# TensorE's program for the twelve later experts of a mixture-of-experts stage, written out in place of a loop of four rounds

## The reference, cut to what matters

```python
y = jnp.zeros_like(h)
for e in range(N_EXPERTS):                         # 16 experts
    a = jax.nn.silu(h @ w_gate[e]) * (h @ w_up[e])  # (t, 1024) @ (1024, 512)
    y = y + gates[:, e:e + 1] * (a @ w_down[e])     # (t, 512) @ (512, 1024)
```

## Time and profile before

| what | value |
|---|---|
| time, three runs | 1175.56, 1176.21, 1176.38 us, median 1176.21 |
| the profiled execution: its own time | 1178.95 us |
| the profiled execution: span, first to last instruction | 1177.1 us |
| mean granted TensorE clock | 0.927 |
| TensorE busy in the span | 983.2 us (84%), of these 368.7 us in the MoE products (L1906) |
| TensorE idle before MoE products, ended by up weights | 47.6 us |
| TensorE idle before MoE products, ended by nothing the profile shows ("issue") | 20.8 us in 12 waits |
| MoE products of layer 0 and of layer 1, in the span | 423.1 to 664.5 us, and 935.3 to 1148.1 us |

### The profile page before, as it was taken

How to read it: one execution, slowest core, us unless ns; L and a number is a source line. 1 busy time by engine, 2 the same in 40 slices (tenths; PEclk the granted TensorE clock), 3 DMA queues, 4 the chain that set the end, 5 groups by cost and what they waited for, 6 DMA issues and landing times.

```text
span 1177.1 us, 24444 instructions
## 1 busy us (share of the span) xinstructions
PE 983.2 (84%) x9596; PEld 652.9 (55%) x9597; DVE 402.6 (34%) x811; ACT 377.5 (32%) x806; POOL 217.6 (18%) x329
## 2 busy tenths in 40 slices
PE   3799999988899989799898569999999779876650
PEld 1477777544555656456566357887555546553430
DVE  1533331357833532122122373123744512121103
ACT  3433321466832222122122354224743112221102
POOL 0000000000000033344344201910000224342211
PEclk8799999999999889899999879999999889997775
DMA  9766664998230749999999467225447698999972
GB/s 340 254 215 217 222 216 176 344 361 322 92 163 36 281 170 372 421 423 422 422 422 399 168 224 169 72 72 187 171 145 312 256 415 354 421 422 425 427 302 113
DMA packets 93682, 322.07 MB, mean 274 GB/s; under 512 B 21241, under 2 KB 33954, under 8 KB 81330
## 3 DMA queue, kind: packets, MB, share of 16 engines
q1 hardware_dynamic: 85746, 305.40, 67.2%
q0 software_dynamic: 7008, 12.62, 2.9%
q10 hardware_dynamic: 864, 3.15, 0.7%
HBM read 313.67 MB, written 13.99 MB: 278 GB/s over the span
## 4 chain that ended last, share of the span: by engine, by line
PE 67%; DMA 17%; DVE 7%; issue 4%; ACT 3%; SPq 1%; POOL 1%; POOLq 0%; DVEq 0%; ACTq 0%
PE ps L1906 23%; PE ps L1667 21%; DMA expert_sets<-in_moe_w_up_dram 10%; PE ps L1822 7%; PE ps L1570 5%; PE ps L1594 4%; DMA ring<-in_ada_w_dram 2%; DMA ada_late<-in_ada_w_dram 2%; DMA expert_rows<-moe,scatter_idx 1%; PE ps L1749 1%; PE ps L1778 1%; PE ps L1722 1%; PE ps L1877 1%; DMA moe<-h_rows,gather_idx 1%; DMA val<-expert_rows 1%
## 5 line engine op out<-in xcount | busy, mean ns | idle before, releaser
L1906 PE MATMUL ps<-expert_sets,moe 128*32 128x256 f32 x6304 | 368.7, 396 | 78.1 <-DMA expert_sets<-in_moe_w_up_dram 47.6
L1906 PEld LDWEIGHTS ps<-expert_sets,moe 128*32 128x32 f32 x6304 | 235.1, 114 | 211.1 <-issue 98.1
L1528 DVE STREAM_TRANSPOSE moe<-moe 128x256 f32<-128x256 f32 x70 | 45.8, 654 | 316.1 <-PE ps L1906 294.2
L1667 PE MATMUL ps<-w_high,x_high 128*128 128x512 f32 x352 | 142.8, 406 | 6.6 <-DVE hT L508 3.0
L1667 PE MATMUL ps<-w_high,x_low 128*128 128x512 f32 x352 | 139.1, 395 | 0.0
L1667 PE MATMUL ps<-w_low,x_high 128*128 128x512 f32 x352 | 139.1, 395 | 0.0
L1083 ACT ACTIVATE moe<-ps 128x128 f32<-128x128 f32 x68 | 18.9, 277 | 261.9 <-PE ps L1906 259.7
L475 DVE TENSOR_TENSOR w_low<-ring,w_high 128x2048 fp32r<-128x2048 f32 x24 | 56.1, 2345 | 132.0 <-ACT w_high L472 132.0
L751 POOL MEMSET moe<- 128x128 f32 x2 | 0.4, 204 | 541.1 <-PE ps L1848 541.1
L774 POOL DMA_INDIRECT expert_rows<-moe,scatter_idx x74 | 75.8, 1024 | 78.7 <-POOL scatter_idx L811 57.9
L1667 PEld LDWEIGHTS ps<-w_high,x_high 128*128 128x128 f32 x352 | 67.4, 191 | 30.6 <-issue 17.4
(11 more groups left out here) (236 smaller groups left out, 1108.7 us busy)
## 6 DMA issues: line engine op xcount, KB each, us to landing
expert_sets<-in_moe_w_down_dram SPq DMA_DIRECT2D x32, 2048.0 KB, 19.3
expert_sets<-in_moe_w_gate_dram SPq DMA_DIRECT2D x30, 2048.0 KB, 18.8
expert_sets<-in_moe_w_up_dram SPq DMA_DIRECT2D x30, 2048.0 KB, 21.8
ring<-in_ada_w_dram SPq DMA_DIRECT2D x16, 2048.0 KB, 8.1
ring<-in_diff_w_qkv_dram SPq DMA_DIRECT2D x6, 2048.0 KB, 8.1
ada_late<-in_ada_w_dram SPq DMA_DIRECT2D x6, 2048.0 KB, 13.0
ring<-in_na_w_qkv_dram SPq DMA_DIRECT2D x6, 2048.0 KB, 8.9
rows<-mod_rows SPq DMA_DIRECT2D x12, 512.0 KB, 8.7
```

The costliest lines, as they stand in the source:

```text
L1528: dve.transpose(blk_inT, blk_in[b].rearrange("p (j k) -> p k j", k=KC)).then_inc(m_xt[l], 1)
L1667: mm = pe.matmul(ps[:, n % 2], x_part[:, k, tok], w_part, start=(k == 0 and i == 0), stop=(k == KC - 1 and i == 2))
L1906: mm = pe.matmul(ps[g * SLOTS:(g + 1) * SLOTS, bank, 0:n_out], lhs_T[:, k, :], weights(k, g), start=(k == 0), stop=(k == n_chunks - 1), sk ...
```

## The change

In TensorE's program, experts 1 to 15 are now all written out with a Python loop that calls `expert` with the number of the expert; the `pe.Fori` of four rounds is gone. The end of an expert's blocks is loaded in the program of the expert before (`then=p + 1`) with a fixed address, and kept in a register of the list `ends`; the two loads at the head of each round are gone. Expert 3, which loaded no end, now loads that of expert 4. `gates_loaded` and `down_loaded` lose their argument `rounds`. The programs of the other four engines are as they were, and so are the products, the weights and their order.

```diff
-                def gates_loaded(p, rounds=0):
+                def gates_loaded(p):
                     nth, per_layer = nth_load(0, p)
                     for w in range(2):
-                        pe.wait_ge(m_wl[gate_set(p)][w], 16 * (nth + rounds + l * per_layer))
+                        pe.wait_ge(m_wl[gate_set(p)][w], 16 * (nth + l * per_layer))
-                def down_loaded(p, rounds=0):
+                def down_loaded(p):
                     nth, per_layer = nth_load(2, p)
-                    pe.wait_ge(m_wl[p % 3][2], 16 * (nth + rounds + l * per_layer))
+                    pe.wait_ge(m_wl[p % 3][2], 16 * (nth + l * per_layer))
-                def expert(p, first, end, rounds=0, then=None):
+                def expert(p, first, end, then=None):
...
-                for p in range(1, 4):
-                    ends.append(expert(p, ends[p - 1], ends[p], then=p + 1 if p < 3 else None))
-                with pe.Fori(0, (N_EXP - 4) // 3) as three:
-                    end_0, end_1 = block_end(3 * three + 3), block_end(3 * three + 4)
-                    end_2 = expert(4, end_0, end_1, three, 3 * three + 5)
-                    end_3 = expert(5, end_1, end_2, three, 3 * three + 6)
-                    expert(6, end_2, end_3, three)
+                for p in range(1, N_EXP):
+                    ends.append(expert(p, ends[p - 1], ends[p], then=p + 1 if p + 1 < N_EXP else None))
```

More of the change, by code:

```diff
@@ L1942, in expert @@
                     else:
-                        gates_loaded(p, rounds)
+                        gates_loaded(p)
                     gates_ups(first, gate_set(p))
                     after = None if then is None else block_end(then)
-                    down_loaded(p - 1, rounds)
+                    down_loaded(p - 1)
                     downs(first - 1, (p - 1) % 3)
                     with pe.If(first + 1 < end):
-                        down_loaded(p, rounds)
+                        down_loaded(p)
                         pe.sem_inc(s_turn_pe, 1)
```

## The result

The changed kernel takes 1186.68 us (median of 4 runs, 1184.25 to 1188.06) against 1176.3 us (1175.56 to 1177.66) for the kernel before: ratio 1.0074, 95% interval 1.0050 to 1.0098. I had predicted 1177.1 and a range up to 1182.0. Single executions of either kernel lie up to 10 us apart, much of it in the stages ahead of layer 0's MoE, which start its stream of weights anywhere between 436 and 444 us.

What follows compares the result with a forecast made beforehand. The stream of weights was taken to end both MoE stages, in layer 1 after TensorE's expert 4. Terms 0 + 0.6 (layer 0) and -0.3 + 0.6 + 0 (layer 1) gave +0.9 us: 1177.1 us, range 1174.2 to 1182.0.

Steps and rivals of the forecast that it cites:

- The heads: Branch and two loads starting each loop round on TensorE; removal worth 0 us, except -0.3 at layer 1's expert 4.
- rivals A and B: A: whole head at layer 1's expert 4 counts, 1174.8 us; B: layer 0's heads too, 1170.4 us; chance 0.08 each.
- rival E: Each of six branches back of the rounds costs a stop for code, so removal saves 16.4 us: 1160.7 us; chance 0.02.
- The packets: 16 KB fetches of TensorE's program; queue q8 was to show 75 of them, not 47.
- an even spread: Added program packets shared by all 16 DMA engines: 0.23 MB at 423 GB/s, 0.54 us a layer.
- More program to fetch: +0.6 us in each layer: 14 more program packets per layer, fetched while the weights' stream is full; +0.6 us each, bounds 0 and 14.6.
- the slower stretch: A layer 1 stretch with three or four program packets, moving 419 GB/s against 423 in the next, without any.
- rival C: Program packets hold up the DMA engine finishing last: 1181 us with four per layer there, 1193 with all; chance 0.12.
- My own sign of being wrong: Gaps in the stream after 1000 us, layer 0's last weights over 2 us off, or line 655's wait ending over 1 us sooner.
- what TensorE gains, it waits longer: Layer 0's heads lie ahead of waits for up weights of 5.66 and 2.65 us, so removing them gives 0 us.
- The stop ahead of expert 4: Layer 1: 2.31 us idle before 968.98, read as a code fetch that stays; head's removal there -0.3, between -2.6 and 0.
- near 998 us: Time when SyncE's wait for TensorE's gates of layer 1's expert 4 was to end, as in the kernel before.

Runs made afterwards that it cites:

- heads_back: The changed kernel with its two loads of block ends put back at the head of every third expert, all still written out; ratio 1.0060 to the kernel before.
- after: The changed kernel, experts 1 to 15 written out in both layers, against the kernel before: ratio 1.0074, in two more measurements 1.0071 and 1.0079.
- before: The unedited kernel with TensorE's loop of four rounds: 1176.3 us; measured again against itself, ratios 0.9994 and 1.0005.
- l1_only: The kernel before with TensorE's program written out in layer 1 only, layer 0 keeping its loop; ratios 1.0032 and 1.0045 in two measurements.
- the two shifted kernels: The kernel before and the changed kernel, each with 128 idle TensorE instructions added at the end of layer 0's MoE; ratios 1.0046 and 1.0058 to the kernel before.

## Why the prediction was wrong

**Right.** The heads are worth nothing in either layer (my 0 and -0.3; heads_back is within 1 us of after), the gains of rivals A and B did not come, and neither did that of rival E. The packets were 75. A head gone turned into a longer stop behind it (2.31 to 4.09 us), as I had argued. Copies of as many bytes cost 0.7 us and less, what I gave for an even spread.

**"More program to fetch: +0.6 us in each layer" was mis-sized: 3.4 us in layer 0, 1.8 in layer 1.** I had two prices for 14 packets, 1.1 us by the slower stretch (0.08 each) and 0.54 by bytes, and took the lower. The mean landing moved by 1.3 us in layer 0 and by 1.0 in layer 1 behind expert 4 (the mean of parts there: 137.0 us in before, 138.0 in after), so about 0.1 us for a packet, near the price that I rejected. And the stage doesn't end with the mean but with the last part, which fell back by another 2.1 us in layer 0 and 0.8 in layer 1, in jumps behind single packets. This is rival C, to which I gave 0.12: not four or five packets on the last engine, but two jumps in layer 0 and one in layer 1, each of 1.3 to 2.0 us, where I had 0.62 us for a packet. My own sign of being wrong, layer 0's last weights over 2 us later, came true. How a packet gets to the engine that is last stays open: l1_only has one such jump in layer 0 without one packet more there.

**A term was missing: the clock.** Where I said "what TensorE gains, it waits longer", I priced the longer wait at nothing. It cost 1.6 us in layer 0, and some 1.5 us in two of the three executions of after behind the stop at expert 4: 657 products took 37.46 us there, and 35.98 in heads_back, where the clock stayed at 1.00. The third kept its clock too, and its expert 4 ended at 59.8 us, 0.6 over the mean of before. The row to price it with was in front of me: 96 products took 7.18 us behind a wait of 7.11 and 5.39 behind one of 2.65.

**The stop ahead of expert 4.** I took its size as given by the next piece of code and the same before and after. By the two shifted kernels it depends on where the code lies in its blocks, which every edit ahead of it in the program moves. Expert 4 ended 1.6 us later on the mean (58.6, 59.7, 59.3 against 61.5, 61.1, 59.8); a shift by half a block alone moves it by 0.5 to 4 us. So the forecast of "near 998 us" could not be had from the trace of before, and should have been a bound of some 3 us upwards, not 0 to -2.6.

**The sum by what was measured**, in place of +0.9: layer 0 +3.4 (landing) +1.6 (clock) = +5.0; layer 1 +1.6 (expert 4, clock in it) +1.8 (landing) +0.4 (its last products and what is behind them, within the scatter of this stage) = +3.8; 8.8 us on 1176.3 is 1185.1, 1.6 us under the 1186.68 of the runs and within their interval.

## What to carry to other kernels

A loop whose body stays at hand (here 4.7 blocks of 16 KB) spares more than its heads cost, when a saturated stream of DMAs ends the stage: here each block of program fetched in it delayed the weights by 0.1 us in the mean of their parts, and some single ones set the last part back by another 1.1 to 2.1 us. Spread bytes of the same amount don't show this price. If a change makes an engine wait longer, look what the products behind a wait of that length cost in the same trace, before the longer wait is put down at nothing. Where TensorE runs new code in short experts, a stop's size hangs on the layout: give it a range from the stops of the whole trace, not the value of its own row.

## What the runs showed of the hardware that I had not expected

- A loop of 9.4 blocks is fetched anew in each round (23 packets in layer 0 instead of 10, 6.84 us at the branch back); one of 4.7 blocks is not.
- 128 idle instructions in a pause of 20.6 us made the kernel before 0.46% slower (0.28 to 0.65), by layout alone; the changed kernel got no slower by them.
- A longer program delays the last part of a transfer in a stage that runs none of the added code: 203.5 and 203.6 us instead of 201.5 to 201.8. Where more program is written out, the last part falls back in single jumps of 1.1 to 2.1 us behind packets that are eight, or a multiple of eight, apart in the program.
- A stop of 5.19 us in one piece left the clock at 0.71 over the next 6.5 us; 1.14 and 2.12 us with 24 products between them left it at 1.00. Not every stop near 3.3 us does so: 3.29 us in the third execution of after left 1.00, 3.46 in the second 0.74.
- An instruction that waits for something long over takes SyncE some 65 ns (17 us for 256).
